# Router of the expert layer: norm weight folded into the router's weights and into an eviction, transposes and gather read the residual rows, root of the mean square in the one-hot

## The reference, cut to what matters

```python
def rms_norm(x, g):
    var = jnp.mean(x * x, axis=-1, keepdims=True)
    return x * lax.rsqrt(var + RMS_EPS) * g

h = h + rms_norm(mixed, p['attn_post_g'])          # norm POST1 of the kernel
xn = rms_norm(h, p['ffn_pre_g'])                   # norm FPRE1
logits = xt @ w_router                             # (256, 1024) x (1024, 8)
top_vals, top_idx = lax.top_k(logits, 2)
top_w = jax.nn.softmax(top_vals, axis=-1)
for e in range(8):
    y = swiglu(xt, w_gate[e], w_up[e], w_down[e])
    out = out + gates[:, e:e + 1] * y
```

## Time and profile before

| | |
|---|---|
| median of 3 runs | 1373.6 us (1372.88 to 1373.73) |
| span of the profiled execution | 1370.5 us |
| PE busy | 1354.9 us, 99% of the span |
| DVE, ACT, POOL busy | 366.8, 293.2, 91.4 us |
| read from HBM | 436.53 MB, 324 GB/s over the span |

### The profile page before, as it was taken

The page is one execution under the profiler, slowest core; times in us unless marked ns, Lnnn a source line. Parts: engine busy times, 40 slices in busy tenths (PEclk is TensorE's granted clock), DMA queues, the critical chain, the costliest instruction groups (busy, mean ns, idle before and its releaser), DMA issues.

```text
span 1370.5 us, 25931 instructions
## 1 busy us (share of the span) xinstructions
PE 1354.9 (99%) x11486; PEld 688.4 (50%) x11486; DVE 366.8 (27%) x417; ACT 293.2 (21%) x403; POOL 91.4 (7%) x226
## 2 busy tenths in 40 slices
PE   9999999999999999999999999999999999999997
PEld 7956888888889853333333333333333333333322
DVE  5765544455555421101101101011010110110111
ACT  5455344434467630010000000000001001001002
POOL 3002000000100062010010000001001001000001
PEclk9999999999999999999999999999999999999999
DMA  8807655555362399999999999999999999999993
GB/s 259 280 32 273 223 192 187 185 184 184 106 233 84 139 405 331 421 415 420 420 417 420 420 418 417 422 417 418 421 418 417 421 418 417 420 420 418 421 380 100
DMA packets 96076, 445.14 MB, mean 325 GB/s; under 512 B 9570, under 2 KB 20002, under 8 KB 63460
## 3 DMA queue, kind: packets, MB, share of 16 engines
q1 hardware_dynamic: 92032, 431.56, 79.9%
q0 software_dynamic: 3936, 11.98, 2.6%
q10 hardware_dynamic: 4, 0.01, 0.0%
HBM read 436.53 MB, written 6.98 MB: 324 GB/s over the span
## 4 chain that ended last, share of the span: by engine, by line
PE 97%; DVE 2%; ACT 0%; issue 0%; DMA 0%; POOL 0%; DVEq 0%; ACTq 0%; POOLq 0%
PE psum L1126 42%; PE psum L1141 14%; PE psum L547 8%; PE psum L549 8%; PE psum L548 8%; PE psum L1145 7%; PE psum L670 2%; PE psum L506 1%; PE psum L529 1%; PE psum L859 1%; PE psum L536 1%; PE psum L850 1%; PE psum L783 0%; DVE reg_a L1685 0%; DVE nmax L1666 0%
## 5 line engine op out<-in xcount | busy, mean ns | idle before, releaser
L1126 PE MATMUL psum<-ring,reg_a 128*32 128x384 f32 (+1 forms) x6144 | 578.8, 539 | 0.0
L1126 PEld LDWEIGHTS psum<-ring,reg_a 128*32 128x32 f32 x6144 | 199.6, 110 | 377.1 <-issue 377.0
L2038 DVE TENSOR_TENSOR work<-memb,psum 128x1152 f32<-128x1152 f32 (+1 forms) x16 | 40.0, 2497 | 518.0 <-PE psum L1126 518.0
L547 PE MATMUL psum<-w_hi,x_hi 128*128 128x512 f32 (+2 forms) x320 | 122.2, 382 | 0.4 <-DVE x_lo L1711 0.2
L1141 PE MATMUL psum<-ring,reg_b 128*32 128x512 f32 x1024 | 121.6, 592 | 0.0
L549 PE MATMUL psum<-w_hi,x_lo 128*128 128x512 f32 (+2 forms) x320 | 120.5, 376 | 0.0
L548 PE MATMUL psum<-w_lo,x_hi 128*128 128x512 f32 (+2 forms) x320 | 120.3, 376 | 0.0
L1716 DVE TENSOR_TENSOR w_lo<-raw,w_hi 128x2048 fp32r<-128x2048 f32 x42 | 96.1, 2290 | 81.9 <-ACT w_hi L1288 81.9
L1551 ACT ACTIVATE memb<-psum 128x1152 f32<-128x1152 f32 (+1 forms) x16 | 20.6, 1290 | 385.8 <-PE psum L1126 385.8
L1288 ACT ACTIVATE w_hi<-raw 128x2048 fp32r<-128x2048 f32 x42 | 80.4, 1916 | 94.1 <-PE psum L549 94.1
L1141 PE MATMUL psum<-ring,reg_a 128*32 128x512 f32 x768 | 91.2, 592 | 0.0
(11 more groups left out here) (304 smaller groups left out, 1143.7 us busy)
## 6 DMA issues: line engine op xcount, KB each, us to landing
ring<-in_l_w_down SPq DMA_DIRECT2D x112, 1024.0 KB, 21.5
ring<-in_l_w_gate SPq DMA_DIRECT2D x64, 1024.0 KB, 21.9
ring<-in_l_w_up SPq DMA_DIRECT2D x64, 1024.0 KB, 21.6
ring<-in_l_w_gate SPq DMA_DIRECT2D x64, 768.0 KB, 20.0
ring<-in_l_w_up SPq DMA_DIRECT2D x64, 768.0 KB, 20.7
raw<-in_l_w_gate SPq DMA_DIRECT2D x14, 1024.0 KB, 5.3
raw<-in_l_w_up SPq DMA_DIRECT2D x14, 1024.0 KB, 5.2
raw<-in_l_w_down SPq DMA_DIRECT2D x14, 1024.0 KB, 5.7
```

What stands on the lines that cost most here:

```text
L547: pe.matmul(out, x[0], w[0], start=first, stop=False, skip_group_check=True)
L1126: ins = pe.matmul(psum[G * c:G * c + G, b0 + g, 0:w], picked[:, g, k, :], x[:, w * c:w * c + w], start=(k == 0), stop=(k == KD - 1), skip_ ...
L2038: dve.tensor_tensor(x.rearrange("p (g c r) -> p g c r", g=NGRP, r=G), act_e[:, 0:NGRP * w].rearrange("p (g r c) -> p g c r", g=NGRP, r=G), ...
```

## The change

Six parts, all in the stretch between attention and experts but for two small loads and one multiplication near the start of the program.

1. FPRE1's gain is multiplied into `wr` once, early (DVE, after two new loads of that gain by SP: `wr_gain` in the layout of `wr`, `row_gain` in the layout of `picked`). So the transposes read `hres` itself, and DVE's multiplications L1942 and L1964 go.
2. The gather's matmuls read `hres` in place of `rows`: their stationary operand is every eighth column of a residual row. ACT's four layouts (L1515) go. The inverse root is put into the one-hot `pick`, now 96 wide, and the gain is applied when `picked` is copied from PSUM: on ACT as four instructions, on DVE as one.
3. The squares of POST1's tile 1 and of FPRE1 are taken in halves of 512 columns (`square_half`), and `mix_late` ends the first half-bank before it starts the last matmuls of the second.
4. The drains of the transposes are shared: ACT takes (0, 1) and (1, 0), DVE (0, 0) and (1, 1). PE's order is now transposes of tile 0, first half of its router, transposes of tile 1, second half of tile 0's router, router of tile 1. Two calls of `keep_running` go and one is shortened.
5. The whole normed rows for `xs` are made by DVE (two instructions) after the table's entries, in place of ACT's L1532.
6. POOL writes `xs`, and loads the last gain, after the table has come back, in place of before `expert_rows`.

The diff, cut to its core:

```diff
-            turn(FPRE1, "f1T", (2, 3), [0])
-            keep_running(5)
-            router_rows(0, 2)
-            keep_running(3)
...
+            def turn_rows(tt, hf, b):
+                if (tt, hf) == (1, 0):
+                    pe.wait_ge(half_added, 1)
                 else:
+                    pe.wait_ge(added, 5 + tt)
...
+                    ins = pe.transpose(bank(b, c * P, (c + 1) * P), hres[:, tt, k * P:(k + 1) * P], ident[:, :])
...
+            for hf in range(2):
+                turn_rows(0, hf, 2 + hf)
+            keep_running(3)
+            pe.wait_ge(wr_ok, 1)
+            router_rows(0, 2, 0)
+            turn_rows(1, 0, 6)
+            turn_rows(1, 1, 7)
+            router_rows(0, 2, 1)
+            router_rows(1, 0, 0)
+            router_rows(1, 0, 1)
             keep_running(4)
...
             for hf in range(2):
-                pe.wait_ge(rows_ok, 2 * NT - 1 + hf)
                 begin(("pre-gather", hf), 4 + hf)
                 for c in range(4):
                     k = 4 * hf + c
                     for tt in range(NT):
-                        ins = pe.matmul(bank(4 + hf, c * CAP, (c + 1) * CAP), rows[:, tt, k * P:(k + 1) * P],
+                        ins = pe.matmul(bank(4 + hf, c * CAP, (c + 1) * CAP),
+                                        hres[:, tt, :].rearrange("p (m c) -> p c m", c=KD)[:, k, :],
                                         pick[:, tt, 0:CAP], start=(tt == 0), stop=(tt == NT - 1))
...
+            def square_half(n, tt, hf, src, ok):
+                cs = slice(hf * 512, (hf + 1) * 512)
+                act.activation(spare[:, tt, cs], src, ACT.Square, scale=D ** -0.5,
+                               accum_out=ssq2[:, n, hf:hf + 1]).then_inc(ok, 1)
 
             post_norm(POST1, 0, ("mix", 1), spare)
...
+            act.wait_ge(added, 5)
+            square_half(3, 0, 0, hres[:, 0, 0:512], whole_squared)
             for hf in range(2):
                 act.wait_ge(*bk.full(("mix", 1, 1, hf)))
...
+                square_half(2, 1, hf, bank(bk.at["mix", 1, 1, hf][0]), half_squared)
+            drain_rows(0, 1)
+            square_half(3, 0, 1, hres[:, 0, 512:1024], whole_squared)
+            drain_rows(1, 0)
+            for hf in range(2):
+                act.wait_ge(half_squared, hf + 1)
+                act.wait_ge(*((half_added, 1) if hf == 0 else (added, 6)))
+                square_half(4, 1, hf, hres[:, 1, hf * 512:(hf + 1) * 512], whole_squared)
...
+            for k in range(4):
+                ins = act.activation(picked[:, :, k, :],
+                                     bank(4, k * CAP, (k + 1) * CAP).rearrange("p (g s) -> p g s", g=NGRP),
+                                     ACT.Copy, scale=row_gain[:, k:k + 1])
...
+            dve.wait_ge(gains_in, 16 * 2)
+            dve.tensor_tensor(wr[:, :, :], wr[:, :, :], wr_gain[:, :].unsqueeze(2).to_broadcast((P, KD, NE)), ALU.mult)\
+                .then_inc(wr_ok, 1)
...
-                ins = dve.tensor_scalar(pick[:, tt, :], iota_s[:, :], rank[:, tt, 0:1], -1.0, ALU.subtract,
-                                        ALU.is_equal)
+                inverse_rms(FPRE1, tt)
+                ins = dve.tensor_scalar(pick[:, tt, 0:CAP], iota_s[:, 1:CAP + 1], rank[:, tt, 0:1],
+                                        rstd[:, FPRE1, tt:tt + 1], ALU.is_equal, ALU.mult)
...
+                for u in range(NT):
+                    pool.wait_ge(scaled_rows, u + 1)
+                    pool.dma_start(xs[u * P:(u + 1) * P, :], xn[:, u, :]).then_inc(rows_out, 16)
+                load_gain(POST1 + NG)
                 pool.wait_ge(rows_out, 16 * NT)
...
+                sp.dma_start(row_gain[:, :], t[NORMS[FPRE1]].rearrange("(p k) -> p k", k=KD)).then_inc(gains_in, 16)
+                sp.dma_start(wr_gain[:, :], t[NORMS[FPRE1]].rearrange("(k p) -> p k", p=P)).then_inc(gains_in, 16)
```

More of the change, by code:

```diff
@@ L1010, in mix_late @@
             def mix_late(tt):
[L1012 to L1018, removed]
+                drained_all(("os", 2), ("os", 3))
+                for hf in range(2):
+                    end(mix_part1(tt, hf, (2, 3)), ("mix", 1, tt, hf))
+                    cut1_free[10 + hf] = bk.full(("mix", 1, tt, hf))
             begin(("mix", 1, 1, 0), MIX1[1])
@@ L1050, in keep_running, with router_rows @@
                               start=True, stop=True, skip_group_check=True)
[L1052 to L1061, removed]
+            def router_rows(tt, b, half):
+                pe.wait_ge(*bk.empty(("f1T", tt, half)))
+                if half == 0:
+                    begin(("logits", tt), b)
+                for k in range(4 * half, 4 * half + 4):
                     ins = pe.matmul(bank(b, 0, 12 * NE).rearrange("p (n e) -> p n e", e=NE),
@@ L1500, in _ @@
             stick_out(3)
[L1502 to L1506, removed]
-            post_norm(POST1, 0, ("mix", 1), spare)
[L1509 to L1517, removed]
@@ L1535, in _ @@
+            for hf in range(2):
+                act.wait_ge(half_squared, hf + 1)
+                act.wait_ge(*((half_added, 1) if hf == 0 else (added, 6)))
+                square_half(4, 1, hf, hres[:, 1, hf * 512:(hf + 1) * 512], whole_squared)
             act.wait_ge(gap_ok, 1)
             act.activation(gate2[:, :, 1:2], gate2[:, :, 0:1], ACT.Exp).then_inc(gexp_ok, 1)
-            copy(("pre-gather", 0), picked.rearrange("p g k s -> p k g s")[:, 0:4],
-                 bank(4, 0, 4 * CAP).rearrange("p (k g s) -> p k g s", k=4, g=NGRP))
+            act.wait_ge(*bk.full(("pre-gather", 0)))
@@ L1961, in _ @@
                     .then_inc(half_added if hf == 0 else added, 1)
-            for hf, cs in enumerate(halves):
-                dve.wait_ge(*((half_added, 1) if hf == 0 else (added, 6)))
-                dve.tensor_tensor(xn[:, 1, cs], hres[:, 1, cs], gains[:, FPRE1 % NG, cs], ALU.mult)\
-                    .then_inc(half_ok if hf == 0 else scaled, 1)
-            dve.wait_ge(scaled, NORM_COUNT[FPRE1, 1])
+            drain_rows(1, 1)
             for tt in range(NT):
@@ L1991, in _ @@
             dve.tensor_tensor(gate2[:, :, 0:1], top_v[:, :, 1:2], top_v[:, :, 0:1], ALU.subtract).then_inc(gap_raw, 1)
-            inverse_rms(FPRE1, NT - 1)
             dve.wait_ge(gap_raw, 1)
@@ L2009, in _ @@
             dve.tensor_copy(job_i[:, :], job_f[:, :]).then_inc(tables_ok, 1)
-            copy(("pre-gather", 1), picked.rearrange("p g k s -> p k g s")[:, 4:8],
-                 bank(5, 0, 4 * CAP).rearrange("p (k g s) -> p k g s", k=4, g=NGRP))
+            dve.wait_ge(*bk.full(("pre-gather", 1)))
+            dve.tensor_tensor(picked.rearrange("p g k s -> p k g s")[:, 4:8],
+                              bank(5, 0, 4 * CAP).rearrange("p (k g s) -> p k g s", k=4, g=NGRP),
+                              row_gain[:, 4:8].unsqueeze(2).unsqueeze(3).to_broadcast((P, 4, NGRP, G)), ALU.mult)\
+                .then_inc(bk.empty_sem(("pre-gather", 1)), 1)
             dve.sem_inc(y_mid, 1)
@@ L2027, in _ @@
             dve.tensor_copy(row_i[:, :, :], row_f[:, :, :]).then_inc(entries_ok, 1)
+            gain_here(FPRE1, 0)
+            for tt in range(NT):
+                dve.scalar_tensor_tensor(out=xn[:, tt, :], in0=hres[:, tt, :], scalar=rstd[:, FPRE1, tt:tt + 1],
+                                         in1=gains[:, FPRE1 % NG, :], op0=ALU.mult, op1=ALU.mult)\
+                    .then_inc(scaled_rows, 1)
             def expert_job(j, last):
```

89 lines of the change are left out of this document (39 added, 50 removed).

## The result

The changed kernel takes 1377.1 us (median of 8 runs, 1376.2 to 1378.6) where the kernel before takes 1372.5 (8 runs, 1372.1 to 1373.7, the three known ahead of the prediction among them): a ratio of 1.0033, 95% interval 1.0024 to 1.0041. It is slower by 4.6 us. The forecast was a microsecond faster, and the range ended at 1376.4: it was wrong, and the side was wrong too.

The account below looks back on a forecast made before the run. The prediction took a relay between engines, in the 14.21 us before the first expert matmul, to bound the kernel. With the gather unchanged, 0.95 and 0.05 off 1373.6 gave 1372.6 us, range 1371.6 to 1376.4.

Parts of the forecast that it names:

- What bounds the kernel: A relay between engines before the first expert matmul sets the end; a microsecond taken out is one of the kernel.
- The relay: Between the last mix matmul and the gather: logits 0.95 us earlier, ranks and one-hot 0.05, together 1.0 less.
- PE's queue: Router instructions queued behind tile 1's transposes on PE: 0.45 of the 1.4 us gained is lost.
- The step on the one-hot: Ranks and one-hot after the logits: `pick`, 96 columns instead of 128, saves some 0.03 us per instruction; 0.05 to 0.1 earlier.
- The step that failed: The gather's 32 matmuls before the experts: stationary columns 32 bytes apart cost nothing, so it stays at 3.81 us.
- strided loads cost: Rival, gather's 32 loads: doubled, 3.8 us more, net 2.8, 1376.4; chance 0.13 for double or more, 0.14 for a part.
- the clock: Rival, before the jobs: fewer unused matmuls and idle PE lower the clock, up to 1380 us; chance 0.02.
- The row from 80 to 85 us: Evidence set against a clock fall: PE busy for 3.90 of 5 us there, granted clock still 1.00.
- The start of the sum: The time counted from: profiled execution 1370.5 us, the median 3.1 above its span, so 1373.6.
- the eviction on ACT: Gain applied after the gather's first half: four instructions, some 1.1 us, covered by the second half's 1.9; costs nothing.
- DVE's product: Gain applied at DVE's copy of `picked`: same size as the copy, wanted some 8 us on; costs nothing.
- The rows `xs`: Rows for the other experts, written 40 us later by POOL: there by about 553, taken at 568.5; nothing on the path.

Follow-up runs that it names:

- e1: The changed kernel, but ACT copies every eighth column of the residual rows together and PE's gather reads the copies: 1371.0 us, ratio 0.9993 to the kernel before.
- e6: e1 with DVE again multiplying tile 1 by FPRE1's gain, unused, before PE may transpose tile 1: 1372.8 us, ratio 0.9997 to the kernel before.
- e7: e1 with DVE's drain of (0, 0) between its gain multiplications and tile 0's whole router before tile 1's transposes: 1371.1 us, ratio 0.9985 to the kernel before.
- e4: The probe: the kernel before plus groups of unused matmuls, stationary or moving operand at steps of 1, 2, 4 and 8 values; 1425.9 us, single run.
- e2: The kernel before, but ACT's copies leave the columns in order and PE's gather reads every eighth: 1377.8 us, ratio 1.0038 to the kernel before.
- e3: The changed kernel with six unused matmuls instead of three ahead of the router: 1376.8 us, ratio 1.0033 to the kernel before.
- e5: The changed kernel with an unused matmul of 512 columns behind each of the gather's 16 matmuls: 1377.7 us, ratio 1.0032 to the kernel before.

## Why the prediction was wrong

**What bounds the kernel**: right. The jobs don't move but for the clock, and the stretch ahead of them shifts the end one for one.

**The relay**: right, to 0.2. Foretold was 1.0 earlier, measured 1.20. The stretch was to be 13.2; the gather made it 17.19, and in e1, without the gather's strided loads, it is 13.02. The residual sum starts 2.17 after the mix (2.3 by the working), the 24 router instructions start 4.16 after it (4.3), and DVE has the logits 7.02 after it (7.35). Of the 0.33 by which the logits are earlier than the working had them, about half comes from a division: the 3.81 holds the tail of the last of 32 instructions, and the trace has them start every 0.112, not 0.119. That the gain is the two multiplications (e6) and that 0.45 of it was left on PE's queue (e7: 0.36) both hold. The step on the one-hot had the wrong sign: its two instructions take 0.57, not less than 0.48. They are narrower, and have a third operand.

**The step that failed is the gather**: "It loads at half of its fastest rate already, so a halving may cost nothing." The price was zero by it and is 4.18. The argument took PE's slow float32 load for spare time in which a slow read could hide. The probe shows that there is none to hide in: the moving operand doubles as well, and so does the float32r load. The faster rate that it was measured against, 512 columns in 0.23, was that of a float32r moving operand (`h_hi`), not of a load. The two neighbours in the trace, ACT at 2.1 ns a column and DVE at 2.0 against 1.2, had it right, and PE's own came to 0.240 us / 128 = 1.9 ns a column, in the probe as in the gather. I had both rows and a rule that fits them, and let a guess about the third engine outweigh them.

**The rival that came**, *strided loads cost*, had the mechanism, the place and the size (3.8 for a doubling, 4.18 measured) at a chance of 0.13 for its full price. Its time of 1376.4 is 0.7 under the median, but it was counted from 1373.6: as a change it was 2.8 slower, where 4.6 was measured. What it lacks is **the clock**, which stood apart as a rival of its own with another cause, fewer fillers and an idle PE. They are one case: the strided loads of this gather, with nothing between them, bring the clock down (e2, e3, e5), and the job behind pays for what is left of the low stretch, 1.1 in e2's profile, 1.8 in e3's and 2.15 in the changed kernel's. The row from 80 to 85 us that I set against a fall, PE busy for 3.90 of 5 and the clock at 1.00, bore out nothing for PE busy all the time with slow loads.

**The start of the sum** was off without harm. Each execution on record with a span of its own took 1.8 to 1.9 longer than its span, so the profiled one of the kernel before, at 1370.5, took about 1372.3. Of the 3.1 set between span and median, 1.3 was that the three first runs were slower than it. The forecast of 1.0 less is not touched by this.

**Nothing, as foretold**: the eviction on ACT starts at 491.51 and is covered by the second half of the gather. DVE's product takes 0.56. The rows `xs`, now issued at 533.0 on POOL's queue, and the gathers of job 1 behind them are in time, as POOL's and DVE's timelines show:

```profile
533.02 1.20 POOL L2248 DMA_DIRECT2D xs<-xn  x2 [0.60 <-POOL recip L2244]
...
547.52 1.06 POOL L2260 DMA_INDIRECT work<-xs,work  x1 [0.37 <-issue]
```

```profile
574.38 1.60 DVE L2057 STREAM_TRANSPOSE reg_a<-work 128x768 f32<-128x768 f32 x1
```

Rows and gathers take 10 and 7 us to land, and DVE takes them 27 after the issue. The second job begins without a wait of PE and lasts 108.20. The covers were larger in the slow gather, but e1 has the same moves without it and a first job of 108.21.

**Open.** The 0.77 by which this one profile's stretch begins later was not traced to a cause. How long the clock stays low differs from one kernel's profile to the next (10.2, 6.8 and 6.8 us). For the executions without a profile there is only the mean granted clock, and it fits a fall in each of them: 0.994 to 0.997 in all 18 of the changed kernel, e2 and e3, 0.998 or 0.999 in all 67 of the kernel before, e1, e5 and e7. One of e6's 11, at 1374.9, has 0.997, and nothing on record says why. How much of the low stretch fell into the job was seen in the profiles alone. A gather whose rows lie two values apart, which the probe prices at almost nothing, was not tried.

## What to carry to other kernels

A copy that "only" lays an operand out can be worth its engine: here four copies on an idle ACT, off the path, save PE 4.18 us of loads and a clock fall. Before PE reads a tile in place, look at the step between neighbouring elements of either operand: in the probe up to 8 bytes was nearly free, and at 16 and 32 bytes the instruction took twice as long. Where the trace has two engines paying double for an access, take that as the price for the third until a probe says otherwise; eight unused matmuls in the kernel settle it.

When operations leave a relay, the in-order queues decide how much arrives: the change kept 1.2 of what the two multiplications gave, and another order of PE's and DVE's queues brought 0.36 more in the trace.

## What the runs showed of the hardware that was not expected

- The price of a strided read on PE is a stair: with a stationary operand of 128 float32 columns an instruction comes every 0.112 us at a step of 4 bytes, 0.118 at 8, 0.233 at 16 and 0.24 at 32, and with a moving one of 128 columns every 0.112, 0.113, 0.227 and 0.233.
- The granted clock fell to 0.50 with PE busy throughout its slow stretch, in each of the four kernels with a run of strided stationary loads and without fillers inside it (the changed kernel, e2, e3, e4), and in none of the three without strided loads (e1, e6, e7) in this stretch. With a matmul of 512 columns behind each pair of strided instructions it held (e5). The probe's slow groups with a strided moving operand did not bring it down; why these differ was not settled, and the transfers had ended by then as well.
- The strided loads themselves came every 0.240 at 1.00 and at 0.50. What the lower level costs shows only on the matmuls behind them, so a profile's slow line and the line that pays for the clock are not the same.
